# Two buffers for the sums of u, and another order on VectorE and ScalarE, in the plain tiles of two FFN layers

## The reference, cut to what matters

```python
def swiglu(u, w_gate, w_up, w_down):
    h = jax.nn.silu(u @ w_gate) * (u @ w_up)      # u: 512 x 1024, w_gate and w_up: 1024 x 2816
    return h @ w_down                             # w_down: 2816 x 1024
...
x = x + swiglu(rmsnorm(x, ffn_norm[i]), ffn_w_gate[i], ffn_w_up[i], ffn_w_down[i])
```

## Time and profile before

| | |
|---|---|
| median of three runs | 1278.86 us (1277.39 to 1279.42) |
| the profiled execution, its own time | 1278.51 us |
| its span, first to last instruction | 1276.7 us |
| TensorE busy | 1225.5 us, 96% of the span |
| VectorE busy | 856.2 us, 67% |
| ScalarE busy | 533.0 us, 42% |
| mean granted TensorE clock | 0.99 of full speed |

### The profile page before, as it was taken

How to read it: one execution, slowest core, us unless ns; L and a number is a source line. 1 busy time by engine, 2 the same in 40 slices (tenths; PEclk the granted TensorE clock), 3 DMA queues, 4 the chain that set the end, 5 groups by cost and what they waited for, 6 DMA issues and landing times.

```text
span 1276.7 us, 18841 instructions
## 1 busy us (share of the span) xinstructions
PE 1225.5 (96%) x7693; PEld 1076.3 (84%) x7693; DVE 856.2 (67%) x1009; ACT 533.0 (42%) x693; POOL 64.0 (5%) x84
## 2 busy tenths in 40 slices
PE   3989997999999999999999999999997999999997
PEld 3778887889988998888888888888877889989986
DVE  8897768568856868746555564634467578857864
ACT  5655545325533545333342234322355335523532
POOL 5940000000000000000000000000000000000000
PEclk9999998999999999999999999999998999999998
DMA  5563332333342333313323132233323333333321
GB/s 115 150 126 100 99 91 75 101 98 100 100 131 67 101 102 112 119 54 108 99 66 107 34 129 76 66 99 99 99 66 99 100 100 100 100 101 98 91 75 66
DMA packets 166521, 121.89 MB, mean 95 GB/s; under 512 B 6104, under 2 KB 158736, under 8 KB 166416
## 3 DMA queue, kind: packets, MB, share of 16 engines
q1 hardware_dynamic: 164784, 118.24, 30.6%
q10 hardware_dynamic: 1664, 2.62, 1.0%
HBM read 114.29 MB, written 2.10 MB: 91 GB/s over the span
## 4 chain that ended last, share of the span: by engine, by line
PE 90%; DVE 4%; ACT 2%; ACTq 1%; issue 1%; DMA 1%; SPq 0%; DVEq 0%
PE bank L821 16%; PE bank L822 16%; PE bank L823 16%; PE bank L876 9%; PE bank L877 9%; PE bank L878 9%; PE bank L1005 2%; PE bank L1003 2%; PE bank L1004 2%; ACTq L519 1%; DMA s<-in_x_dram 1%; PE bank L717 1%; PE bank L1031 1%; PE bank L1032 1%; PE bank L1033 1%
## 5 line engine op out<-in xcount | busy, mean ns | idle before, releaser
L1096 ACT ACTIVATE w_hi<-w_raw 128x2048 fp32r<-128x2048 f32 (+1 forms) x70 | 130.4, 1863 | 172.8 <-PE bank L823 154.0
L821 PE MATMUL bank<-u_hi,w_hi 128*128 128x512 f32 x480 | 188.5, 393 | 0.0
L822 PE MATMUL bank<-u_lo,w_hi 128*128 128x512 f32 x480 | 186.8, 389 | 0.0
L823 PE MATMUL bank<-u_hi,w_lo 128*128 128x512 f32 x480 | 186.8, 389 | 0.0
L1510 DVE TENSOR_TENSOR w_lo<-w_raw,w_hi 128x2048 fp32r<-128x2048 f32 x46 | 105.4, 2290 | 60.7 <-ACT w_hi L1096 60.5
L1500 DVE TENSOR_TENSOR tmp<-bank,tmp 128x512 f32<-128x512 f32 (+2 forms) x118 | 77.8, 659 | 88.2 <-PE bank L823 53.1
L876 PE MATMUL bank<-s_hi,w_hi 128*128 128x256 f32 x408 | 116.0, 284 | 0.0
L877 PE MATMUL bank<-s_lo,w_hi 128*128 128x256 f32 x408 | 115.9, 284 | 0.0
L878 PE MATMUL bank<-s_hi,w_lo 128*128 128x256 f32 x408 | 115.8, 284 | 0.0
L821 PE MATMUL bank<-hid_hi,w_hi 128*128 128x512 f32 x288 | 113.0, 392 | 0.9 <-issue 0.9
L822 PE MATMUL bank<-hid_lo,w_hi 128*128 128x512 f32 x288 | 112.2, 389 | 0.0
(11 more groups left out here) (274 smaller groups left out, 2725.3 us busy)
## 6 DMA issues: line engine op xcount, KB each, us to landing
w_raw<-in_ret_w_qkvg_dram SPq DMA_DIRECT2D x24, 1024.0 KB, 5.0
w_raw<-in_ffn_w_up_dram SPq DMA_DIRECT2D x44, 512.0 KB, 3.7
w_raw<-in_ffn_w_gate_dram SPq DMA_DIRECT2D x44, 512.0 KB, 4.8
w_raw<-in_ffn_w_down_dram SPq DMA_DIRECT2D x16, 1024.0 KB, 5.0
w_raw<-in_ret_w_o_dram SPq DMA_DIRECT2D x8, 1024.0 KB, 5.2
w_raw<-in_ffn_w_down_dram SPq DMA_DIRECT2D x8, 768.0 KB, 4.4
w_raw<-in_s_glu_w_dram SPq DMA_DIRECT2D x4, 1024.0 KB, 5.2
s<-in_x_dram ACTq DMA_DIRECT2D x8, 256.0 KB, 8.1
```

What stands on the lines that cost most here:

```text
L821: pe.matmul(o, w_hi[w][:, w_cols], hi, start=first, stop=False)
L822: pe.matmul(o, w_hi[w][:, w_cols], lo, start=False, stop=False)
L823: return pe.matmul(o, w_lo[w][:, w_cols], hi, start=False, stop=end)
L1096: return act.activation(o, i, ACT.Copy, scale=scale)
```

## The change

The instructions are the same ones in number and size; what changes is the place of buffers, some waits, and the order on ScalarE and VectorE in units 1 to 4 of each layer.

- `s_raw`, `a_raw` and `b_raw` get two buffers each, by k % 2. `scaled_u` and `u_sums` of k then wait for the work of k - 2 instead of k - 1. The two `s_raw` lie over `r_hi0` and part of `r_lo0` (before: over `r_lo0`), so the first rounding and subtraction of raw weights in buffer 0 (unit 6) wait for the last `s_split`; the same wait falls away for the others. The second `a_raw` and `b_raw` lie over hidden tile 4.
- In unit 1, both engines do unit 2's weights first, ahead of `root` and `inverse_rms`; `scaled_u` for k = 0 and 1 follows. `hidden(0)` moves from unit 1's list to unit 2's, behind `gate_out(1)`; `hidden_low(1)` moves to unit 3's list behind `gate_out(2)`.
- In units 2 and 3 the next unit's weights come first on ScalarE; on VectorE they follow the outputs of the unit before.
- `sums` of unit 5 move from unit 4's list to the end of unit 3's; `raw_high` of unit 5 comes first on ScalarE in unit 4; `raw_low` and `sum_low` come ahead of the last `u_sums_low`.

```diff
-        s_raw = sb(lap, "s_raw", [P, 4, HALF])
+        s_raw = sb(lap, "s_raw", [P, 2, 4, HALF])
...
-        a_raw = sb(over, "a_raw", [P, SEQ])
+        a_raw = sb(over, "a_raw", [P, 2, SEQ])
...
             def scaled_u(layer, k, gain_col):
-                if k:
-                    act.wait_ge(s_raw_ready, KH * layer + k)
+                if k > 1:
+                    act.wait_ge(s_raw_ready, KH * layer + k - 1)
...
             def raw_high(layer, n):
...
+                if unit.z == 0 and s == 0:
+                    act.wait_ge(s_split, KH * (layer + 1))
...
# ScalarE, chunked_hidden, unit.kind == "C", n > 0
+                        if kind(n + 1) == "C":
+                            plain_high(layer, n + 1)
+                        else:
+                            raw_high(layer, n + 1)
                         if n == 1:
                             root(norm)
-                            high(n + 1)
+                            scaled_u(layer, 0, gain_col)
+                            scaled_u(layer, 1, gain_col)
                             silu(n - 1)
-                            hidden_high(n - 1)
                             continue
+                        if n == 2:
+                            u_sums_high(layer, 0)
+                            hidden_high(n - 2)
                         silu(n - 1)
-                        ks = FACTORS_AT[n]
...
+                        if n < KH:
+                            scaled_u(layer, n, gain_col)
+                        else:
+                            sum_high(layer, n + 1, 0)
+                            sum_high(layer, n + 1, 1)
+                        u_sums_high(layer, n - 1)
                         hidden_high(n - 1)
...
# VectorE
             def u_sums(layer, k):
...
-                if k:
-                    dve.wait_ge(s_split, KH * layer + k)
+                if k > 1:
+                    dve.wait_ge(s_split, KH * layer + k - 1)
...
             def raw_low(layer, n):
-                dve.wait_ge(s_split, KH * (layer + 1))
+                if unit.z == 0 and s == 0:
+                    dve.wait_ge(s_split, KH * (layer + 1))
...
# VectorE, chunked_hidden, unit.kind == "C", n > 0
                         if n == 1:
+                            split_weights(0, pair + 1)
                             inverse_rms(norm)
                             clear_sum()
+                            gate_out(n - 1)
+                            u_sums(layer, 0)
+                            continue
                         gate_out(n - 1)
...
+                        if n == 2:
+                            hidden(n - 2)
+                        elif n == 3:
+                            hidden_low(n - 2)
+                        if kind(n + 1) == "C":
+                            split_weights((n + 1) % 2, PAIR0[f"ffn{layer}"] + (n + 1) // 2)
+                            u_sums(layer, n - 1)
+                            if n == 2:
+                                u_sums_low(layer, 0)
+                                hidden_low(n - 2)
+                                hidden(n - 1)
+                                continue
                             hidden(n - 1)
+                            u_sums_low(layer, n - 2)
                             hidden_low(n - 1)
+                            sums(layer, n + 2, 0)
+                            sums(layer, n + 2, 1)
                             continue
...
+                        u_sums(layer, n - 1)
+                        raw_low(layer, n + 1)
                         hidden(n - 1)
...
+                        u_sums_low(layer, n - 2)
+                        sum_low(layer, n + 1)
+                        u_sums_low(layer, n - 1)
                         hidden_low(n - 1)
```

More of the change, by code:

```diff
@@ L182 @@
 NORM_BANK = [2, 7, 2, 7]
-FACTORS_AT = {2: (0,), 3: (1, 2), 4: (3,)}
 def wide_free(layer, n, m):
@@ L317, in trunk @@
         r_lo1 = sb(over, "r_lo1", [P, 3 * PART], F32R)
+        lap = ExitStack()
+        s_raw = sb(lap, "s_raw", [P, 2, 4, HALF])
+        lap.close()
         r_hi0 = sb(over, "r_hi0", [P, 3 * PART], F32R)
-        lap = ExitStack()
-        s_raw = sb(lap, "s_raw", [P, 4, HALF])
-        lap.close()
         r_lo0 = sb(over, "r_lo0", [P, 3 * PART], F32R)
@@ L325, in trunk @@
         over = ExitStack()
-        sb(over, "below_a_raw", [P, 2 * KT * SEQ + 2 * KH * 4 * HALF + 5 * SEQ])
-        a_raw = sb(over, "a_raw", [P, SEQ])
-        sb(over, "below_b_raw", [P, 5 * SEQ])
-        b_raw = sb(over, "b_raw", [P, SEQ])
+        sb(over, "below_a_raw", [P, 2 * KT * SEQ + 2 * KH * 4 * HALF + 4 * SEQ])
+        a_raw = sb(over, "a_raw", [P, 2, SEQ])
+        sb(over, "below_b_raw", [P, 4 * SEQ])
+        b_raw = sb(over, "b_raw", [P, 2, SEQ])
         over.close()
@@ L1257, in scaled_u @@
             def scaled_u(layer, k, gain_col):
-                if k:
-                    act.wait_ge(s_raw_ready, KH * layer + k)
+                if k > 1:
+                    act.wait_ge(s_raw_ready, KH * layer + k - 1)
                 for o, t in ((a_raw, k), (b_raw, KH + k)):
-                    last = act.activation(o[:, :], xT[:, t, :], ACT.Copy, scale=vecs[:, gain_col + t:gain_col + t + 1])
+                    last = act.activation(o[:, k % 2, :], xT[:, t, :], ACT.Copy, scale=vecs[:, gain_col + t:gain_col + t + 1])
                 last.then_inc(a_ready, 1)
@@ L1794, in u_sums @@
             def u_sums(layer, k):
+                raw, a, b = s_raw[:, k % 2, :, :], a_raw[:, k % 2, :], b_raw[:, k % 2, :]
                 dve.wait_ge(a_ready, KH * layer + k + 1)
-                if k:
-                    dve.wait_ge(s_split, KH * layer + k)
-                dve.tensor_tensor(s_raw[:, 3, :], a_raw[:, 0:HALF], a_raw[:, HALF:SEQ], ALU.subtract)
-                step(dve.tensor_tensor(s_raw[:, 0, :], a_raw[:, HALF:SEQ], b_raw[:, HALF:SEQ], ALU.add))
+                if k > 1:
+                    dve.wait_ge(s_split, KH * layer + k - 1)
+                dve.tensor_tensor(raw[:, 3, :], a[:, 0:HALF], a[:, HALF:SEQ], ALU.subtract)
+                step(dve.tensor_tensor(raw[:, 0, :], a[:, HALF:SEQ], b[:, HALF:SEQ], ALU.add))
                 settle()
-                step(dve.tensor_tensor(s_raw[:, 1, :], s_raw[:, 0, :], a_raw[:, 0:HALF], ALU.subtract))
+                step(dve.tensor_tensor(raw[:, 1, :], raw[:, 0, :], a[:, 0:HALF], ALU.subtract))
                 settle()
-                dve.tensor_tensor(s_raw[:, 2, :], b_raw[:, 0:HALF], s_raw[:, 1, :], ALU.subtract).then_inc(s_raw_ready, 1)
+                dve.tensor_tensor(raw[:, 2, :], b[:, 0:HALF], raw[:, 1, :], ALU.subtract).then_inc(s_raw_ready, 1)
             def u_sums_low(layer, k):
                 dve.wait_ge(s_hi_ready, KH * layer + k + 1)
-                dve.tensor_tensor(s_lo[:, k, :, :], s_raw[:, :, :], s_hi[:, k, :, :].bitcast(F32),
+                dve.tensor_tensor(s_lo[:, k, :, :], s_raw[:, k % 2, :, :], s_hi[:, k, :, :].bitcast(F32),
                                   ALU.subtract).then_inc(s_split, 1)
@@ L1910, in next_norm @@
                             add_square(norm + 1, t)
[L1912 to L1921, removed]
                 for n, unit in enumerate(UNITS):
@@ L1936, in chunked_hidden @@
                             hidden_low(n - 1)
+                            sums(layer, n + 2, 0)
+                            sums(layer, n + 2, 1)
                             continue
[L1938 to L1942, removed]
-                        hidden(n - 1)
[L1944 to L1951, removed]
@@ L1952, in chunked_hidden @@
-                        prepare(n + 1)
+                        u_sums(layer, n - 1)
+                        raw_low(layer, n + 1)
+                        hidden(n - 1)
+                        u_sums_low(layer, n - 2)
+                        sum_low(layer, n + 1)
+                        u_sums_low(layer, n - 1)
                         hidden_low(n - 1)
-                        for k in ks[1:]:
-                            u_sums_low(layer, k - 1)
-                            u_sums(layer, k)
```

17 lines of the change are left out of this document (1 added, 16 removed).

## The result

| | before | changed |
|---|---|---|
| median of the runs | 1278.34 us (1277.39 to 1279.42) | 1260.3 us (1258.36 to 1261.03) |
| the profiled execution, time and span | 1278.51, 1276.7 | 1260.84, 1259.1 |
| TensorE busy | 1225.5 us (96%) | 1219.4 us (97%) |
| mean granted TensorE clock | 0.990 | 0.996 |

The ratio is 0.9856, 95% interval 0.9839 to 0.9873: 18.0 us less by the medians, 17.7 between the two profiled executions. The forecast was 15.9 us less, 1262.9, with a range of 1260.0 to 1266.8.

The account below looks back on a forecast made before the run. TensorE, busy 96%, bounds the kernel, so only its waits and the low clock behind them can pay: 2 x (9.66 - 1.7) = 15.9 us less, 1278.51 to 1262.6, median 1262.9, range 1260.0 to 1266.8.

Parts of the forecast that it names:

- The stall and the order of work: In front of units 5 and 4: 7.65 and 0.27 us lost a layer go; unit 5's w_lo about 2.2 us early.
- Two figures in hand: Unit 5's w_lo ready 8.3 to 8.7 us after unit 3's end; unit 4's weights with 6.5 us in hand.
- The covers: Root and reciprocal (over 2 us in hand), banks of units 3 and 4, and unit 6: each costs nothing.
- The new wait in front of unit 2: Unit 2 waits for the bank hidden(0) frees: 1.54 us lost, 1.7 us a layer with the restart.
- Rival B: Unit 2 doesn't wait for its bank: the full 19.3 us gained, 1259.5; chance 0.05.
- The rule that the forecast set beside its own price: VectorE's next operation waits for an empty pipe: hidden(0) 0.09 us later, sum 0.2 us higher for both layers.
- The low clock behind the stall: Behind unit 5's stall, 18 matmuls at about half clock: 1.74 us a layer lost, which goes with the stall.
- The low clock outside the stalls: Kernel end, clock 0.50: no term in the sum; a microsecond or two allowed in the forecast's own range, 1261.0 to 1264.5.
- Rival C: Unit 2's new idle of 1.4 us lowers the clock, 1.8 us in a layer: 1264.7 to 1266.5; chance 0.10.
- the argument against it: At 25 to 28 us TensorE stood still 1.7 us of 3, clock 1.00; with 7.5 us it fell.
- E: Clock falls before unit 2 and stays low through plain units: slower, 1282 for a whole unit of 48; chance 0.03.

Follow-up runs that it names:

- experiment 7: Changed kernel with hidden(0) back in unit 1's list, and root, reciprocal, clear_sum and gate_out(0) ahead of unit 2's weights again: 1256.52 us.
- Experiment 5: Changed kernel with hidden(0) put behind the sums of u for k = 1 as well, lengthening unit 2's wait: 1268.02 us in a single execution.
- experiments 1 and 3: 1: changed kernel with hidden(0) back in unit 1's list, 1257.27 us; 3: kernel before with only unit 4's lists reordered, one buffer, 1265.66 us.
- fourth profile of before: The kernel before, nothing changed, profiled a fourth time: 1278.76 us, one execution.
- third profile: The kernel before, nothing changed, profiled a third time: 1279.1 us, one execution.
- second of before: The kernel before, nothing changed, profiled a second time: 1278.29 us, one execution.

## Where the prediction was right, and the step that failed

**The stall and the order of work: right.** The 7.65 us in front of unit 5 and the 0.27 in front of unit 4 went in both layers. `w_lo` was over 2.8 us early instead of 2.2; the lists had been added up without overlap. (Two figures in hand don't follow from the forecast's own terms: 8.3 plus at most 0.2 late is 8.5 us, not 8.7, and unit 4's weights have 10.9 - 4.2 = 6.7 us in hand, not 6.5. Neither enters the sum.) The covers held where nothing was charged: root and reciprocal (experiment 7), the banks of units 3 and 4 and unit 6, none of which shows a wait.

**The new wait in front of unit 2: right**, in its place, its cause and its size. Forecast 1.54 us of wait and 1.7 with the restart; measured a step of 1.86 us instead of 0.23, so 1.63, and 1.75 by undoing it. Before unit 5 the stretch shrank by 6.2 us a layer, where the forecast's terms give 7.65 + 0.27 - 1.7 = 6.22. Rival B is out. The rule that the forecast set beside its own price does not describe these rows: `gate_out(1)` and `hidden(0)` took 1.29 us together, less than 0.69 + 0.68. The section of the Trainium skill that it named ("VectorE: DVE Perf Modes", "The DRAIN you can't avoid") itself says that a next operation that is not held starts earlier, and that is what these rows show.

**The low clock behind the stall: mis-sized.** The forecast took 1.74 us a layer from one execution. Over four profiles of before and eight stalls it is 1.38 to 2.77, mean 1.97. By all seven profiles of the two kernels the stretches behind unit 5 shrank by 1.95 us in either layer. The two layers together then give 2 x 6.2 + 3.9 = 16.3 us, not 15.9.

**The low clock outside the stalls: the step that failed.** The forecast's sum carries everything but the two stretches over unchanged: "the profiled execution's 1278.51 becomes 1262.6, and the median of the runs, 0.35 above it, 1262.9". That puts the change of low clock elsewhere at nothing, and it allowed "a microsecond or two" for it in its own range alone. The first half came out: the profiled executions (1278.67 on average before, 1262.14 changed) differ by 16.5, as the layers say. The second half did not. The changed kernel's median is 0.5 us below its first profiled execution instead of 0.35 above, and the medians moved by 17.9 to 18.0, which is 1.6 more than the two layers explain.

What differs in the other executions is the granted clock. The three profiled ones of the changed kernel have a mean of 0.995 or 0.996, which is 10 to 13 us of low clock in the whole execution; the six others have 0.996 to 0.999 (1258.36 us twice at 0.999, so about 2.5 us: 0.001 x 2 x 1256.6). In the profile of before the clock is low in these stretches, beside the last 1.6 us:

```profile
203.40:210.20 6.80, 3.75 (x17) 3.75 (x18) 6.73 (x8) 2.37 (x4) 0.00 (x0) 0.50 0.38 113
961.20:967.90 6.70, 3.89 (x18) 3.89 (x19) 6.63 (x8) 2.28 (x3) 0.00 (x0) 0.50 0.42 121
1261.60:1271.70 10.10, 9.97 (x47) 9.57 (x47) 2.58 (x6) 3.07 (x6) 0.00 (x0) 0.50 0.10 39
```

That is 25.5 us; without the two at the stalls, some 12 are left, and that is what the forecast carried over. An estimate from the clocks: the six other executions have 0.9975 on average, so some 6 us of low clock, about 5.5 less; at half speed that is 2.8 us of time, enough for what is missing. Where it lies no trace shows, since these executions have no profile. The end is the likeliest place: in all thirteen profiles of this case it takes 10.1, 11.7 to 11.8 or 13.1 to 13.3 us, by how long the clock is low in it, and in the profiles at hand that is no better in the changed kernel (10.1 to 13.3 in four of before, 11.8 to 13.3 in three of the changed). The start takes 142.5 to 144.0 us in the changed kernel and 143.0 to 143.6 before, and does not explain it either. No execution of before had a mean clock over 0.991. Why the changed kernel's other executions have less low clock was not found; that it is chance among few executions is not excluded.

**Rival C, the clock behind the new gap: it did not happen, but the argument against it was unsound.** The forecast put 1.7 us of idle with the clock kept, at 25 to 28 us, against 7.5 with the clock lost, and gave it 0.10. The row does say 1.00, but TensorE's own steps there say otherwise: eight transposes took 1.97 us, where eight of the same shape took 1.09 a little later, and they follow each other by 0.21 us, as those at the end of the kernel do at 0.50.

```profile
21.20 1.95 PE L687 MATMUL bank<-ident,s_states 128*128 128x128 f32 x8
26.71 1.97 PE L643 MATMUL bank<-ident,s_w 128*128 128x128 f32 x8 [3.56 <-DVE s_w L1637]
28.47 5.73 PE L693 MATMUL bank<-ident,s 128*128 128x128 f32 x32
38.24 1.09 PE L643 MATMUL bank<-ident,s_w 128*128 128x128 f32 x8
```

The clock was at half on both sides of an idle spell of 3.56 us, and rose while the 32 of the third row ran. So this row says nothing of what a gap does. The trace did hold a spell of the right size, which the forecast didn't use: 1.39 us of idle at 85 us, with the clock at 1.00 from 83 to 89. It also held 2.63 us at the end of the kernel, with low clock behind it. The outcome was as forecast, but not for the reason given. Experiment 5 shows the clock lost in both layers at 3.06 us; another 1.6 us on VectorE in front of `hidden(0)` cost 3.1 us a layer instead of 1.6. **E**, low clock through whole plain units, has no support: 7 slow steps behind the 3.06 us gap in layer 0.

## What to carry to other kernels

When an engine's list is reordered so that urgent work comes first, look at each step that moves behind a wait: `hidden(0)` was not late for its own reader, but it frees the bank that the next unit opens, and behind `gate_out(1)` it could only run when that unit should already have started. A long stall in front of one unit can have two repairs that overlap: here the order of the last unit's list alone brought 12.8 us, everything else without it 15.6, both together 17.9. What one of them is worth depends on whether the other is in, so test each alone. A clock column is to be held against the steps of equal instructions before an argument rests on it. And a gain of 1% is read from matmul-to-matmul stretches, which repeat to 0.04 us, rather than from whole times, which vary by 5 us with the granted clock.

## What was not expected of the hardware

- Between matmuls of 512 columns, 3.06 us of idle TensorE lowered the clock in two of two cases, 1.47 us in none of six (three profiles of the changed kernel). In one case it fell only 1.4 us after the matmuls had started again.
- How long TensorE idles does not by itself decide. In the start of the kernel it waits around 78 us in eleven of the thirteen profiles, for 1.5 to 2.4 us. In three of them the clock was low behind that, after 2.05, 1.86 and 2.02 us, in experiments 1 and 3 and the fourth profile of before; after 2.44 us, in its third profile, it was not. The same 32 matmuls there, fourth profile and third:

```profile
79.72 3.37 PE L717 MATMUL bank<-s_tc,s_fb 64*16 64x128 f32 x32 [2.02 <-POOL s_tc L2257]
```

```profile
80.02 1.92 PE L717 MATMUL bank<-s_tc,s_fb 64*16 64x128 f32 x32 [2.44 <-POOL s_tc L2257]
```

- The same stall was followed by 13 to 28 matmuls at the lower clock, from execution to execution.
- At the end of the kernel, behind 2.6 us of idle, the clock fell in all thirteen profiles and stayed low for 3.4 to 10.2 us, with TensorE shown as fully busy. Windows of the first profile of the changed kernel and of the second of before:

```profile
1244.90:1246.40 1.50, 1.50 (x14) 1.50 (x15) 0.32 (x1) 0.63 (x1) 0.00 (x0) 1.00 0.00 0
1246.40:1253.60 7.20, 7.20 (x37) 7.00 (x35) 2.19 (x4) 2.69 (x5) 0.00 (x0) 0.53 0.07 28
```

```profile
1264.00:1271.00 7.00, 7.00 (x35) 6.94 (x34) 2.15 (x4) 2.68 (x5) 0.00 (x0) 0.50 0.07 28
```
